# Finer loads at both ends of the expert stage, an earlier table load, a split subtraction and fewer idle products in a two-block fp32 model

## The reference, cut to what matters

```python
def expert_block(args):
    x_blk, e = args
    return (jax.nn.silu(x_blk @ w_gate[e]) * (x_blk @ w_up[e])) @ w_down[e]
...
x = (x + g2 * y).astype(x.dtype)
return rms_norm(x, final_g)
...
def swiglu(x, w_in, w_out):
    gate, up = jnp.split(x @ w_in, 2, axis=-1)
    return (jax.nn.silu(gate) * up) @ w_out
...
x = x + 0.5 * swiglu(rmsnorm(x, ffn1_norm_g[l]), ffn1_w_in[l], ffn1_w_out[l])
```

## Time and profile before

| what | us |
|---|---|
| median of 3 runs | 1280.64 |
| lowest and highest of them | 1277.49, 1282.91 |
| the profiled execution | 1280.48 |
| its span | 1278.7 |
| PE busy in the span | 1074.8 (84%) |
| DVE, ACT, POOL busy | 515.3, 402.7, 39.8 |

### The profile page before, as it was taken

One profiled execution on the slowest core, in us unless ns is written; L12 is line 12 of the kernel. 1 busy time (PEld: TensorE's weight loads), 2 busy tenths in 40 slices (PEclk: granted clock), 3 DMA queues, 4 the chain that ended last, 5 costly groups with the idle time before them and its releaser, 6 DMA issues.

```text
span 1278.7 us, 16448 instructions
## 1 busy us (share of the span) xinstructions
PE 1074.8 (84%) x7234; PEld 814.6 (64%) x7234; DVE 515.3 (40%) x608; ACT 402.7 (31%) x482; POOL 39.8 (3%) x69
## 2 busy tenths in 40 slices
PE   6999999465656472747789999999999999999998
PEld 4995594222222130313389999889887778999986
DVE  3554541201102020202165555357744786555443
ACT  2435632000000000000053444346644535444432
POOL 1001200000000000000000000000000220000000
PEclk9999899877888787969899999999999999999999
DMA  9997888999999999999955655455454354665430
GB/s 366 307 356 288 326 306 356 428 428 428 426 427 428 429 427 426 427 425 421 395 187 188 196 198 188 141 195 210 148 198 137 127 197 148 198 198 198 177 120 33
DMA packets 110754, 358.17 MB, mean 280 GB/s; under 512 B 8388, under 2 KB 56152, under 8 KB 95320
## 3 DMA queue, kind: packets, MB, share of 16 engines
q1 hardware_dynamic: 109048, 353.63, 71.7%
q10 hardware_dynamic: 1632, 3.45, 0.8%
HBM read 356.01 MB, written 1.05 MB: 279 GB/s over the span
## 4 chain that ended last, share of the span: by engine, by line
PE 69%; DMA 23%; DVE 3%; ACT 1%; issue 1%; SPq 1%; POOL 0%; DVEq 0%; ACTq 0%
PE psum L1941 17%; PE psum L1942 17%; PE psum L1943 17%; DMA spare<-in_moe_w_down_dram 7%; DMA ring<-in_moe_w_down_dram 5%; PE psum L2224 4%; PE psum L2255 3%; DMA ring<-in_moe_w_gate_dram 2%; DMA spare<-in_moe_w_gate_dram 2%; DMA ring<-in_moe_w_up_dram 2%; DMA spare<-in_moe_w_up_dram 2%; DMA ring<-in_ada_w_dram 2%; PE psum L2213 2%; PE psum L1893 1%; PE psum L2174 1%
## 5 line engine op out<-in xcount | busy, mean ns | idle before, releaser
L1565 DVE TENSOR_TENSOR wl<-ring,wh 128x2048 fp32r<-128x2048 f32 x102 | 234.2, 2301 | 231.0 <-ACT wh L1057 230.9
L1057 ACT ACTIVATE wh<-ring 128x2048 fp32r<-128x2048 f32 x102 | 195.1, 1916 | 307.3 <-PE psum L1943 289.0
L1941 PE MATMUL psum<-hTh,wh 128*128 128x256 f32 x832 | 235.2, 283 | 0.0
L1942 PE MATMUL psum<-hTl,wh 128*128 128x256 f32 x832 | 234.9, 282 | 0.0
L1943 PE MATMUL psum<-hTh,wl 128*128 128x256 f32 x832 | 234.7, 282 | 0.0
L1941 PEld LDWEIGHTS psum<-hTh,wh 128*128 128x128 f32 x832 | 158.7, 191 | 0.2
L1943 PEld LDWEIGHTS psum<-hTh,wl 128*128 128x128 f32 x832 | 158.7, 191 | 0.0
L1942 PEld LDWEIGHTS psum<-hTl,wh 128*128 128x128 f32 x832 | 158.6, 191 | 0.0
L2224 PE MATMUL psum<-ring,m_xT 128*32 128x512 f32 x448 | 95.9, 653 | 64.4 <-DMA spare<-in_moe_w_up_dram 50.6
L2224 PEld LDWEIGHTS psum<-ring,m_xT 128*32 128x32 f32 x448 | 25.4, 120 | 117.4 <-issue 116.6
L1524 DVE TENSOR_TENSOR m_h<-m_sg,psum 128x512 f32<-128x512 f32 x8 | 8.2, 1028 | 212.5 <-PE psum L2224 172.2
(11 more groups left out here) (346 smaller groups left out, 1612.0 us busy)
## 6 DMA issues: line engine op xcount, KB each, us to landing
ring<-in_ffn_w_in_dram SPq DMA_DIRECT2D x44, 1024.0 KB, 7.8
ring<-in_moe_w_down_dram SPq DMA_DIRECT2D x16, 2048.0 KB, 32.5
ring<-in_w_mix_in_dram SPq DMA_DIRECT2D x32, 1024.0 KB, 6.2
ring<-in_moe_w_gate_dram SPq DMA_DIRECT2D x15, 2048.0 KB, 29.3
ring<-in_moe_w_up_dram SPq DMA_DIRECT2D x13, 2048.0 KB, 29.4
ring<-in_ada_w_dram SPq DMA_DIRECT2D x24, 1024.0 KB, 12.7
spare<-in_moe_w_up_dram SPq DMA_DIRECT2D x11, 2048.0 KB, 32.2
ring<-in_ffn_w_out_dram SPq DMA_DIRECT2D x20, 1024.0 KB, 6.1
```

The source lines that it names most:

```text
L1057: a.activation(dst, src, ACT.Copy).then_inc(split_h, 1)
L1565: v.tensor_tensor(split_half(h, wl), raw_half(h), split_half(h, wh).bitcast(FP32), ALU.subtract)\
L1941: t.matmul(dst, sh, mh, start=first, stop=False, skip_group_check=True)
L1942: t.matmul(dst, sh, ml, start=False, stop=False, skip_group_check=True)
```

## The change

1. **First freed slots.** A new loader `down_row` brings one row kk of a down unit for its two experts: 128 partitions by 2 runs of 4 KB, 1 MB in all. Units 10 and 11 come as four such loads: row 0 of both as soon as PE has used kk of 0 and 1 of units 0 and 1 (a new semaphore `first_rows_used`), row 1 of both when it has used the rest.
2. **Last two units.** Units 94 and 95 come as four such loads: row 0 of both, then row 1 of both. PE's wait for the units now covers row 0, and it waits for `last_row` ahead of kk of 1.
3. **Table load.** ACT loads the square root's table set right after the last group's copies, ahead of the branch (and back and forth in the branch that isn't taken), instead of in `two_norms`.
4. **First FFN weight.** DVE makes the rest of the first half unit in two pieces of 128x1024: gate at the old place, up after the rests of the transposed parts. PE waits for `first_gate` ahead of the half unit, and for `split_l` ahead of its up products.
5. **Idle products.** 12, 16, 2, 2, 2 and 5 become 4, 3, 1, 1, 1 and 1. Seven stand ahead of the first transposes, where 28 stood.

The branch that isn't taken now counts on the semaphores `wa_in` instead of its own.

```diff
         def landed_count(n):
-            return sum(16 if whole(m // UNITS_PER_GROUP) else 32 for m in range(n % RING_E, n + 1, RING_E))
+            landed = sum(16 if whole(m // UNITS_PER_GROUP) else 32 for m in range(n % RING_E, n + 1, RING_E))
+            return landed if n < expert_total - 2 else landed - 16
...
-            for n in range(expert_total):
+            def down_row(n, row, landed):
+
+                g, u = n // UNITS_PER_GROUP, n % UNITS_PER_GROUP
+                dst = slots_e[n % RING_E][0].rearrange("p (e k n) -> p e k n", e=2, k=2)
+                e, lo = g * EG + 2 * (u % 2), 2 * D * ((u - KD) // 2) + D * row
+                sp.dma_start(dst[:, :, row, :], down_v[:, e:e + 2, lo:lo + D]).then_inc(landed, 16)
+
+            for n in range(expert_total - 2):
...
                     sp.dma_start(gain1, row(ffn1_norm_g[0])).then_inc(gain_in[3], 16)
+                    for r in range(2):
+                        for i in range(2):
+                            sp.wait_ge(main.used if r else first_rows_used, i + 1)
+                            down_row(n + i, r, we_in[(n + i) % RING_E])
+                if n in (RING_E, RING_E + 1):
+                    continue
...
+            for i in range(2):
+                n = expert_total - 2 + i
+                sp.wait_ge(main.used, n - RING_E + 1)
+                down_row(n, 0, we_in[n % RING_E])
+            for i in range(2):
+                down_row(expert_total - 2 + i, 1, last_row[i])
...
             def two_norms():
 
-                a.preload_act_table_set("sqrt_and_others")
...
                 expert_copies(g, main)
+            a.preload_act_table_set("sqrt_and_others")
             act.wait_ge(r_done, 1)
...
+            def split_first(w, done):
+
+                dve.wait_ge(split_h, 1)
+                v.tensor_tensor(split_half(0, wl)[:, :, w, :], raw_half(0)[:, :, w, :],
+                                split_half(0, wh).bitcast(FP32)[:, :, w, :], ALU.subtract).then_inc(done, 1)
+                given[0] = 1
...
-            split_to(1)
+            split_first(0, first_gate)
...
                 rest_of_hT(2, tt, half)
+            split_first(1, split_l)
...
                             if kk == 3 and e % 2 == 1:
                                 last.then_inc(S.used, 1)
+                            if S is main and it == 0 and u == 0 and kk == 1 and e % 2 == 1:
+                                last.then_inc(first_rows_used, 1)
...
                         f = u + kk
+                        if S is main and it == NEG - 1 and f == KF_E - 1:
+                            for row_in in last_row:
+                                pe.wait_ge(row_in, 16)
...
-            keep_busy(psum[:, 7, :], 12)
+            keep_busy(psum[:, 7, :], 4)
             pe.wait_ge(main.acc, NEG + 1)
 
             for tt, half in order_of(2):
-                turn(2, tt, half, 16 if (tt, half) == (0, 0) else 2)
+                turn(2, tt, half, 3 if (tt, half) == (0, 0) else 1)
...
                         for i, kind in enumerate(("gate", "up")):
+                            if h == 0 and i == 1:
+                                pe.wait_ge(split_l, 1)
...
-            keep_busy(open_bank(pe, ("gate", 0, 0)), 5)
+            keep_busy(open_bank(pe, ("gate", 0, 0)), 1)
             ffn(0)
```

More of the change, by code:

```diff
@@ L429, in build_program @@
         main, over = Experts("moe", 0), Experts("over", RING_A)
-        over_in = [sem(f"over{s}_in") for s in range(RING_A)]
+        first_rows_used, first_gate = sem("first_rows_used"), sem("first_gate_rest")
+        last_row = [sem(f"last_row{i}_landed") for i in range(2)]
         def await_unit_used(eng, unit):
@@ L721, in _ @@
                                 sp.wait_ge(over.used, (r * NEG + g) * UNITS_PER_GROUP + (u + 1))
-                                expert_unit(u, g * EG, slot_a(u), over_in[u % RING_A])
+                                expert_unit(u, g * EG, slot_a(u), wa_in[u % RING_A])
                     sp.end_ifs()
@@ L1030, in _ @@
             with act.If(longest > CAP):
+                a.preload_act_table_set("silu_and_others")
                 with act.Fori(0, ROUNDS - 1) as r:
@@ L1928, in next_half @@
                 h = taken[1]
-                pe.wait_ge(split_l, h + 1)
+                if h:
+                    pe.wait_ge(split_l, h + 1)
+                else:
+                    pe.wait_ge(first_gate, 1)
                 taken[1] += 1
@@ L2198, in landed_units @@
                             flat = slot_a(v)
-                            pe.wait_ge(over_in[v % RING_A], it * 32 + 16 * (v // RING_A + 1))
+                            front = 32 * len(range(v % RING_A, NA, RING_A))
+                            pe.wait_ge(wa_in[v % RING_A], it * 32 + (front + 16 * (v // RING_A + 1)))
                         if merged:
```

## The result

The changed kernel takes **1270.57 us** (median of 5, 1268.96 to 1273.71) against 1278.76 us for the kernel before in the same measurement (median of 5, 1277.05 to 1282.91): ratio 0.9934, 95% interval 0.9918 to 0.9949. That is 8.2 us less where 8.5 were forecast. A second measurement, with 5 and 9 runs, gave 1270.52 against 1278.57 us, ratio 0.9951 (0.9937 to 0.9965); the quotient of its two medians, 0.9937, lies at the lower end of that interval.

What follows compares the result with a forecast made beforehand. The expert stage was taken as bound by its weight stream, the FFN by PE. Terms along the chain between them brought the second half unit 8.5 us sooner: 1280.5 - 8.5 = 1272.0 us, range 1268.5 to 1275.5.

Steps and rivals of the forecast that it cites:

- The first freed slots: Start of the expert weight stream: SP's load goes after the 6th product instead of the 14th, -1.7 us.
- Rival 3: Expert stream: early loads are worth nothing, FFN weight's landing does not move; -7.4 us, 1273.1 us, chance 0.08.
- Runs of 4 KB: Row loads at the stream's head and tail: 4 KB runs move slower than 8 KB ones, +0.6 us.
- The last two units: Behind the last expert landing: 16 records stand in place of 32, -1.8 us for x.
- The table load: ACT before the squares: load goes into the wait for the FFN weight; squares start 2.4 us sooner, shift included.
- the split subtraction: DVE in the norm: a smaller piece of the subtraction holds back the first root's use less, -1.05 us.
- The idle products and the hole: PE's transposes: fewer idle products, instruction stop kept until 645.7 us; fourth transposes near 646.2 instead of 654.51 us.
- The wait of 0.6 us for DVE ahead of the second half unit: FFN start: the second half unit waits 0.6 us for DVE and starts at 654.3 us.
- Rival 1: Transposes: no instruction stop, PE runs as DVE allows; -9.5 us, 1271.0 us, chance 0.25.
- Rival 2: FFN start: first products run at half clock, costing 1.6 us; 1273.6 us, chance 0.15.
- Rivals 4 and 5: Seam between experts and FFN held elsewhere, 1279.4 us, chance 0.05; row loads break the stream, 1290.7 us, chance 0.03.
- One sign of being wrong: FFN: the stretch behind 663 us taking longer than before would show the prediction wrong.

Runs made afterwards that it cites:

- u1: Changed kernel with the loads of the first freed slots put back as before the change; 1270.79 us in one run.
- u2: Changed kernel with the last two units loaded and multiplied as before the change; 1272.63 us in one run.
- pad16: Changed kernel with 16 never-executed idle products added in the branch that isn't taken, moving later instructions to higher addresses; 1275.31 us in one run.
- pad8: Changed kernel with 8 never-executed idle products added in the branch that isn't taken; 1277.81 us in one run.
- order: Changed kernel with DVE's new x put behind the first split of the second half's weight instead of ahead of it; 1269.34 us in one run.
- u3: Changed kernel with the table load put back to its old place ahead of the squares; 1273.33 us in one run.
- b_idle: Kernel before the change with only the idle products reduced as in the change; 1271.20 us in one run.
- u4: Changed kernel with the first FFN weight's subtraction whole and at its old place; 1275.51 us in one run.
- u5: Changed kernel with as many idle products ahead of and between the transposes as before the change; 1274.90 us in one run.
- best: Changed kernel with the edits of pad16 and order together; median of 5 runs 1269.25 us.

## Why the prediction was right, by its own steps

- **The first freed slots, -1.7:** right. SP's load comes 1.72 us sooner behind the first product; A fell by 1.52 from before to changed, and by 1.67 when u1 is the comparison. Rival 3 is out.
- **Runs of 4 KB, +0.6:** wrong. At the tail u2 shows 0.2 or less (A 429.86 without them, 429.79 to 430.08 with them). At the head, A's shift of 1.52 to 1.67 leaves 0.1 to 0.2 of the 1.74. I took the rate of the first 16 us, 410 GB/s in the earlier trace rows; by these runs that rate isn't the price of the run length, and what made it isn't shown. The Trainium skill (DMA: Bandwidth & Descriptors, Specifications), by which runs of 512 B and more are at line rate, gave 0 for this term and was the better guide here. For the stretch at 347 GB/s with its shorter runs the two still don't agree, and no experiment here took that up.
- **The last two units, -1.8:** right, 1.72 (B). The term's note that 0.5 of it wouldn't be collected at the squares came true in part: the squares start 0.60 behind x and not 0.31 as before, but `hn` loses only 0.07 us by it (7.86 against 7.79 in u2, pad16, pad8 and order, where they start 0.3 behind x).
- **The table load, -2.4 with the shift, and the split subtraction, -1.05:** right for `hn`, which was ready at 644.65, and worth nothing for the kernel as far as the runs go: u3 takes the table load out, b_idle has neither. What both are worth together, with x as early as in the changed kernel, wasn't run; by the estimate at u4 it is some 0.5 us or more. This the prediction had in its numbers, without drawing it out: it let PE stand until 645.7 and had `hn` at 645.15. By its own numbers the table load at its old place would put `hn` at 646.45 against fourth transposes at 646.2, and cost 0.25 us and not 1.3. u3 shows 0.04 us for 1.43 us of later `hn`, and b_idle that the idle products alone are 0.7 us better behind x than the whole change.
- **The idle products and the hole:** right, the main term and its size. The fourth transposes came 0.4 us later than forecast (646.58 against 646.2): the rest of PE's instructions was there 6.28 us after the restart instead of 6.0. The count of 28 records was off by two, 26 in the changed kernel, so the stop fell ahead of the third transposes, and not in them. That all of C's gain comes with this edit the prediction didn't say; b_idle and u5 do.
- **The wait of 0.6 us for DVE ahead of the second half unit:** right in kind, 0.38 us (6.21 from the first product to the second half unit, against 5.83 in u4 and b_idle), and `order` takes it away.
- **Rival 1 (no hole)** didn't come true, but pad16 makes it true: 1.3 us, forecast 1.0. The Trainium skill (Runtime: NRT & Kernel Launch, Instruction fetch mechanics) has blocks refilled while the engine works, so that a crossing is mostly hidden. The runs show where it isn't: the first crossing behind the branch with which PE jumps over the second pass, if it is reached sooner than about 9 us after x, which is 6 us after PE goes on.
- **Rival 2 (the clock stays low)** didn't come true in the changed kernel, where the clock was half from 639.7 to 643.1 us and full in the FFN. It didn't in any trace here: in u4 the clock was half to 650.7 us and in pad8 to 652.8, through the transposes, but full again at the first product (652.07 and 653.91). The price is paid ahead of the FFN, about 2.6 us in pad8 (C 4.2 us longer, where the stop alone had 1.6).
- **Rivals 4 and 5** are out: the seam moved by 8.4 us, and the stream moved 427 GB/s as before.
- **One sign of being wrong came true in the profiled run:** from the second half unit to the end are 617.5 us against 615.8 before. 1.6 of that is the dip near 895 us; in best, which doesn't have it, the stretch takes 615.8 us. So the FFN's later part is not slower by the change.

So the total was right partly by luck: 0.6 of cost that wasn't there stands against a stop that ended 0.3 later and a start 0.28 us later in the profiled run.

## What to carry to other kernels

When several edits shorten roads that meet at one wait, each has to be tried against the late one: here fewer idle products alone gave 6.2 us behind x, and two others beside them gave nothing that one run shows (the table load in u3, the split subtraction in b_idle), because PE stood waiting for instructions until after they were done. What is hidden behind one stop has to be tried again once the stop is gone. Idle products that fill a wait have to be counted again whenever that wait gets shorter. And where single traces start at different times and dip at different places, compare intervals between two events of the stage in question, not their times; with those, one trace told 0.3 us apart where the five times of one kernel lie 3 to 6 us apart.

## What the runs showed of the hardware

- **The stop behind a branch has a second part.** PE stands for 3.6 us where it jumps over the second pass; then it runs until it comes to a certain address, and if that is before 8.9 to 9.2 us behind x, 6.0 to 6.3 us after its restart (before 8.88, changed 9.14, u1 9.03, u3 9.17, u5 9.07, pad8 8.91), it stops until then. Pushing the instructions on by products in a branch that isn't taken moved the stop by exactly their records (8 products: 26 to 10), and 16 products took it out of the way: 1.3 us for code that never runs.
- **In one kernel (u2) the fetch came 1.2 to 1.4 us sooner**, 4.93 us after the first and not 6.13 to 6.35, and the stop was hidden. This isn't explained.
- **The granted clock differs between runs of the same program** by when it falls to half, not only by how much: the changed kernel has a stretch of 6.8 us at half clock at 141 to 149 us in one trace and none in the other, and its first group starts 3.4 us later for it (199.69 against 196.33). Two more such places come and go from one kernel's trace to the next: 1.6 us near 895 us, 1.2 to 1.9 us at the last expert unit. That no edit causes these is argued from where the edits lie; no two traces of the same program differ in them.
